# The mask product of the banded heads: identity and band held in one float32r tile, written once by ScalarE

## The reference

```python
def gqa_sink_attend(q, k, v, mask, sinks):
    s = jnp.einsum('bqkgd,bnkd->bkgqn', qg, k).astype(jnp.float32) * (HEAD_DIM ** -0.5)
    if mask is not None:
        s = jnp.where(mask, s, NEG_INF)        # NEG_INF = -1e30
    ...
    p = jax.nn.softmax(jnp.concatenate([s, sink], axis=-1), axis=-1)[..., :-1]
    o = jnp.einsum('bkgqn,bnkd->bqkgd', p.astype(v.dtype), v)
```

## Time and profile before

| | us |
|---|---|
| median of 3 runs | 3647.12 (3645.98 to 3649.39) |
| the profiled execution: its own time | 3649.55 |
| the profiled execution: span | 3647.8 |
| TensorE busy | 3357.4 (92%) |
| VectorE busy | 2337.5 (64%) |
| ScalarE busy | 1849.9 (51%) |

### The profile page before, as it was taken

One profiled execution on the slowest core, in us unless ns is written; L12 is line 12 of the kernel. 1 busy time (PEld: TensorE's weight loads), 2 busy tenths in 40 slices (PEclk: granted clock), 3 DMA queues, 4 the chain that ended last, 5 costly groups with the idle time before them and its releaser, 6 DMA issues.

```text
span 3647.8 us, 56528 instructions
## 1 busy us (share of the span) xinstructions
PE 3357.4 (92%) x24411; PEld 3080.7 (84%) x24411; DVE 2337.5 (64%) x2986; ACT 1849.9 (51%) x2198; POOL 0.2 (0%) x4
## 2 busy tenths in 40 slices
PE   7979999989689899999999999898799979998798
PEld 7968989989689799999999999775577869974598
DVE  6756655567566588888888888534465545555354
ACT  5454444445544377777776776423444434434343
POOL 0000000000000000000000000000000000000000
PEclk9989999999899899999999999997799989999899
DMA  6423455444234599899899998323224355411253
GB/s 248 163 86 114 171 211 193 173 162 152 93 116 171 200 372 352 330 353 349 329 360 336 342 360 324 129 78 127 104 87 157 127 198 184 174 59 58 93 185 116
DMA packets 102671, 723.49 MB, mean 198 GB/s; under 512 B 11664, under 2 KB 13328, under 8 KB 16528
## 3 DMA queue, kind: packets, MB, share of 16 engines
q1 hardware_dynamic: 102416, 719.80, 53.2%
HBM read 718.71 MB, written 1.05 MB: 197 GB/s over the span
## 4 chain that ended last, share of the span: by engine, by line
PE 80%; DVE 9%; ACT 6%; DMA 3%; issue 1%; SPq 0%; DVEq 0%; ACTq 0%
PE PS L1361 14%; PE PS L1362 13%; PE PS L1363 13%; PE PS L1314 6%; PE PS L1312 6%; PE PS L1313 6%; DVE WL L2064 3%; PE PS L1618 3%; PE PS L1616 3%; PE PS L1617 3%; ACT WH L1680 3%; PE PS L1428 3%; PE PS L1457 2%; DMA RAW<-in_ffn_w 1%; PE PS L1391 1%
## 5 line engine op out<-in xcount | busy, mean ns | idle before, releaser
L2064 DVE TENSOR_TENSOR WL<-RAW,WH 128x2048 fp32r<-128x2048 f32 (+3 forms) x428 | 962.9, 2252 | 646.7 <-ACT WH L1680 641.5
L1680 ACT ACTIVATE WH<-RAW 128x2048 fp32r<-128x2048 f32 (+3 forms) x428 | 802.7, 1878 | 270.3 <-PE PS L1363 182.0
L1361 PE MATMUL PS<-PH,WH 128*128 128x256 f32 x2464 | 715.5, 290 | 34.8 <-DVE PL L2236 11.1
L1362 PE MATMUL PS<-PL,WH 128*128 128x256 f32 x2464 | 700.9, 284 | 0.0
L1363 PE MATMUL PS<-PH,WL 128*128 128x256 f32 x2464 | 700.7, 284 | 0.0
L2064 DVE TENSOR_TENSOR WL<-F,WH 128x2048 fp32r<-128x2048 f32 x210 | 481.2, 2292 | 87.5 <-ACT WH L1680 86.5
L1361 PE MATMUL PS<-HPH,WH 128*128 128x256 f32 (+1 forms) x1648 | 496.9, 302 | 41.7 <-DVE WL L2064 27.1
L1361 PEld LDWEIGHTS PS<-PH,WH 128*128 128x128 f32 x2464 | 475.3, 193 | 43.8 <-issue 29.8
L1362 PE MATMUL PS<-HPL,WH 128*128 128x256 f32 (+1 forms) x1648 | 482.4, 293 | 0.0
L1363 PE MATMUL PS<-HPH,WL 128*128 128x256 f32 (+1 forms) x1648 | 482.3, 293 | 0.0
L1362 PEld LDWEIGHTS PS<-PL,WH 128*128 128x128 f32 x2464 | 475.2, 193 | 1.3
(11 more groups left out here) (379 smaller groups left out, 5158.4 us busy)
## 6 DMA issues: line engine op xcount, KB each, us to landing
F<-in_moe_w SPq DMA_DIRECT2D x210, 1024.0 KB, 5.1
RAW<-in_ffn_w SPq DMA_DIRECT2D x130, 1024.0 KB, 4.8
RAW<-in_moe_w SPq DMA_DIRECT2D x126, 1024.0 KB, 4.9
RAW<-in_w_in SPq DMA_DIRECT2D x64, 1024.0 KB, 4.8
F<-in_ada_w SPq DMA_DIRECT2D x18, 1024.0 KB, 11.2
RAW<-in_ada_w SPq DMA_DIRECT2D x18, 1024.0 KB, 5.9
RAW<-in_w_kv SPq DMA_DIRECT2D x16, 1024.0 KB, 4.7
RAW<-in_w_in_ab SPq DMA_DIRECT2D x12, 1024.0 KB, 4.9
```

Source lines behind the costliest of these rows:

```text
L1361: T_.matmul(out, lh, rh, start=first, stop=False)
L1362: T_.matmul(out, lh, rl, start=False, stop=False)
L1680: S.activation(mem["WH"][:, t.s % NHL, 0:m], v.raws[t.slot][:, 0:m], ACT.Copy).then_inc(*ac.done("w_hi", t.s))
L2064: V.tensor_tensor(mem["WL"][:, t.s % NHL, 0:m], v.raws[t.slot][:, 0:m], mem["WH"][:, t.s % NHL, 0:m].bitcast(F32), sub).then_inc(*dv.done( ...
```

## The change

The band gets an input tensor of its own and is no longer part of `CST2`. SyncE loads it into the tile `BIAS`, which no head uses yet. In `lam2` ScalarE waits for it and writes a new tile `BAND` of type float32r: columns 0 to 127 eight times the identity, columns 128 to 639 the band. The banded heads' mask product reads both operands from there as float32r. The neighbourhood heads' product reads the same identity reinterpreted as float32, and stays a float32 product with the float32 bias. The first two bias loads and the first mask or bias product wait for `band_r`. The masked value is -2^100 in place of -1e30. `CST2` shrinks by 640 columns and `BAND`, next to it, has 640.

```diff
-CONSTS2 = [("ident8", 128), ("rot", 128), ("cos", 256), ("sin", 256), ("band", 512)]
+CONSTS2 = [("rot", 128), ("cos", 256), ("sin", 256)]
@@ the loads of the neighbourhood heads' biases
-   after=() if hd > 1 else [("ps", "v", f"d0.{i}") for i in range(4)] + [("ps", "v", f"n0.{i}") for i in range(8)])
+   after=() if hd > 1 else [("ps", "v", f"d0.{i}") for i in range(4)] + [("ps", "v", f"n0.{i}") for i in range(8)] + [("band_r",)])
@@ tensor_program, s
         if spec["bias"]:
+            pe.wait_ge("band_r")
             if spec["kind"] == "near":
                 tile = plan.tile["bias", spec["hd"]]
                 pe.wait_ge(f"land{tile.slot}", tile.turn)
                 b = tile.raw[:, 0, qb * T:qb * T + T]
             else:
-                b = v.C2("band")[:, qb * T:qb * T + T]
-            last = T_.matmul(ps[:, 256:512], v.C2("ident8"), b, start=False, stop=True)
+                b = mem["BAND"][:, 128 + qb * T:128 + qb * T + T]
+            eight = mem["BAND"][:, 0:128]
+            last = T_.matmul(ps[:, 256:512], eight.bitcast(F32) if spec["kind"] == "near" else eight, b, start=False, stop=True)
@@ scalar_program, lam2
     def lam2():
+        ac.wait_ge("band")
+        S.activation(mem["BAND"][:, 0:128], v.C("ident"), ACT.Copy, scale=8.0)
+        S.activation(mem["BAND"][:, 128:640], mem["BIAS"][:, :], ACT.Copy).then_inc(*ac.done("band_r"))
         ac.wait_ge("lam2_s")
@@ sync_program, second
         SP.dma_start(mem["CST2"][:, :], io["cst2"]).then_inc(*sp.done("cst2", by=16))
+        SP.dma_start(mem["BIAS"][:, :], io["band"]).then_inc(*sp.done("band", by=16))
         SP.dma_start(mem["LAMB"][:, :], io["lamb"]).then_inc(*sp.done("lamb", by=16))
@@ build
         mem["CST2"] = sb("CST2", [128, NCST2])
+        mem["BAND"] = sb("BAND", [128, 640], F32R)
@@ constants
-    band = np.concatenate([np.where(np.abs(q * 128 + p[:, None] - j[None, :]) <= 128, 0.0, NEG) for q in range(2)], 1).astype(np.float32)
+    band = np.concatenate([np.where(np.abs(q * 128 + p[:, None] - j[None, :]) <= 128, 0.0, -2.0 ** 100) for q in range(2)], 1).astype(np.float32)
```

More of the change, by code:

```diff
@@ L623, in splits_ahead @@
         if t.after:
-            newest = max(newest, *(at[x[1:]] if x[0] == "ps" and x[1] != "v" else at["pair", "mg1"] if x[1] == "mg1" else -1 for x in t.after))
+            newest = max(newest, *(-1 if x[0] == "band_r" else at[x[1:]] if x[0] == "ps" and x[1] != "v" else at["pair", "mg1"] if x[1] == "mg1" else -1 for x in t.after))
         if t.split:
@@ L2748, in constants @@
     cos, sin = (np.tile(f(ang).T, (2, 1)).astype(np.float32) for f in (np.cos, np.sin))
-    band = np.concatenate([np.where(np.abs(q * 128 + p[:, None] - j[None, :]) <= 128, 0.0, NEG) for q in range(2)], 1).astype(np.float32)
+    band = np.concatenate([np.where(np.abs(q * 128 + p[:, None] - j[None, :]) <= 128, 0.0, -2.0 ** 100) for q in range(2)], 1).astype(np.float32)
     iota = np.concatenate([np.tile(np.arange(128.0), (128, 1)), p[:, None], p[:, None] + 128.0], 1).astype(np.float32)
-    return cst, causal, np.concatenate([ident * 8, rot, cos, sin, band], 1), iota
+    return cst, causal, np.concatenate([rot, cos, sin], 1), band, iota
 def lay_out(x):
@@ L2776, in lay_out @@
     par["ml_rows"] = rows
-    cst, causal, cst2, iota = constants()
+    cst, causal, cst2, band, iota = constants()
     wc = x["w_in_c_2"][0]
@@ L2794, in lay_out @@
     out = {
-        "par": np.concatenate([par[n] for n, _ in VECS], 1), "cst": cst, "causal": causal, "cst2": cst2, "iota": iota,
+        "par": np.concatenate([par[n] for n, _ in VECS], 1), "cst": cst, "causal": causal, "cst2": cst2, "band": band, "iota": iota,
         "xT": packed(x["x"][0].T)[0], "memT": packed(x["mem"][0].T)[0], "ctxT": packed(x["ctx_2"][0].T)[0],
```

## The result

The changed kernel took 3635.37 us (median of 7 runs, 3631.26 to 3639.21), the kernel before 3649.39 us in its 7 runs beside it (3645.98 to 3653.93). The ratio is 0.9962, with a 95% interval from 0.9951 to 0.9974. A second comparison on another chip gave 3635.43 us (12 runs) against 3643.14 us (35 runs), ratio 0.9976 (0.9965 to 0.9986). So the change makes the kernel 0.2 to 0.4% faster, 9 to 14 us; the forecast was 9.8 us. The two intervals overlap. The changed kernel had the same time in both, and the runs of before differ by 6 us; whether that is chance or the chip, no run tells.

A forecast was written before the change was run, and what follows sets the result against it. TensorE, busy 92% of the span, was taken as the bound. 10.9 us saved on mask products, less 0.1 for `lam2` and 1.0 for the clock, gave 9.8 off 3647.12: 3637.3 us, range 3631 to 3644 (forecast case alone 3634 to 3640).

The forecast's parts named there:

- The price of a product: Banded mask product on TensorE: from 0.63 to 0.32 us at full clock, saving 0.31, or 0.65 at the lower clock.
- Rival (a): Banded mask product: float32r alone between float32 products costs more, saving 0.23 us each, 7.4 us, 3640.8 us; chance 0.08.
- (e): Banded mask product still has two records, or its 0.63 us stay: 3647.2 us; chance 0.04.
- All on the path: Banded heads: all 32 mask products stand on the chain, so their 10.9 us of saving counts in full.
- Rival (b): Banded heads: a new wait takes half the gain, leaving 4.3 us, 3642.8 us; chance 0.12.
- The clock: Banded stage: slightly more time at the lower clock takes back 1 us, between nothing and 3.5.
- Rival (c): Banded stage: one stretch of lower clock fewer, gain 14.3 us, 3632.8 us; chance 0.13.
- (d): Banded stage drops to the differential heads' clock; slower, 3654.2 us with six more low-clock stretches; chance 0.05.
- `lam2`: ScalarE's two copies, 0.92 us, go into 0.83 us of idle time ahead of the exponential: 0.1 us added.
- Loads and waits: One more DMA ahead of `lamb` and new waits for `band` and `band_r`: costed at nothing, uncovered some 4 us each.

The follow-up runs named there:

- two multiplied kernels: The runs five float32r and three float32, which issue the banded mask product several times: 3652.74 us, and ratio 1.0064 to the kernel before.
- five float32r: Changed kernel with the banded mask product issued five times instead of once, all float32r: 3652.74 us, ratio 1.0023 to the kernel before.
- again: Same kernel rerun without edit: changed, ratio 0.9976 to before; before, ratio 0.9992; type undone, for its profile, banded stage 159.34 us.
- more copies: Changed kernel with four more ScalarE copies of 128x512 ahead of the two in `lam2`: 3636.04 us, ratio 0.9975.
- near_copies: near_r with all its copies, moves and waits, but the neighbourhood heads' product still float32: 3642.56 us, ratio 1.0.
- near_r: Changed kernel extended to the neighbourhood heads: ScalarE copies each bias to float32r, their 16 products are float32r too: 3638.46 us, ratio 0.9995.
- type undone: Changed kernel with the banded mask product reading BAND as float32 again, copies, loads, waits and mask value kept: 3646.09 us, ratio 1.001.
- -1e30: Changed kernel with the masked value at -1e30 again, rounded to float32r by ScalarE: 3637.48 us, ratio 0.9979.
- mask over 128 columns: Changed kernel with the banded mask product over only the 128 columns holding anything but zero: one profile, 0.26 us on the chain.
- three float32: Changed kernel with the banded mask product in float32 and issued three times: ratio 1.0064 to the kernel before, stage 186.75 us.
- no mask: Changed kernel without the banded heads' mask product at all: 3619.58 us, ratio 0.9931.

## Why the prediction was right

**The price of a product** was right to 0.01 us: 0.315 for 0.32 at the full clock, 0.51 for 0.50 at the lower. The two multiplied kernels gave its parts separately, 0.215 us for a float32 record and 0.117 for a float32r one. The other 0.20 us were there in both kernels; how they divide between the weight load and the change from 64 rows to 128 and back, no run separates. Rival (a), a dearer lone record, is out, and so is (e).

**All on the path** was right. In the first part of the stage, up to 3290 us on the clock of before, neither kernel met the lower clock. Eleven mask products lie there, and the changed kernel was 3.5 us ahead: 11 x 0.315. In the same part five float32r records cost 5.2 us over one (11 x 4 x 0.117), and six float32 records 9.5 us over two (11 x 4 x 0.215), both in full. The chain has 24 of the 32 products in the changed kernel where it had all 32, so a few are now beside VectorE's and ScalarE's steps, but these steps had waited for a product themselves. Rival (b) is out: its 4.3 us lie below both intervals of the gain, and the runs with more records show it from the other side.

**The clock** was the term that I had too small in the profiles of this stage. 10.9 us of work went and the stage got 7.3 us shorter, where I had expected about 10. The granted clock went from 0.91 of 160.5 us to 0.89 of 153.2, and since only the levels 1.2 and 2.4 GHz occur, that is 29 us at the lower one before and 34 after. 5 us more at half speed cost up to 2.5; the traces' own clock marks (27.3 and 34.1 us) make it 3.4. I had allowed 1.0 with 3.5 as the end. It was alike in four profiles of kernels with this stage (153.2 to 153.5 us at 0.89: changed, again, with more copies, near_copies), so it is no single accident, but near_r, whose banded stage has the same TensorE work, had 149.6 us at 0.92. The sign is therefore not a law, and that less work causes more of the lower clock is argued, not shown.

The length of the stage in all these kernels, the time at the lower clock in it by the marks, and the length less half of that time. If TensorE were all that counts, the last column would be the length at the full clock:

| kernel | us | us at the lower clock | length less half of them |
|---|---|---|---|
| before, again | 160.5, 160.5 | 27.3, 27.3 | 146.8, 146.9 |
| type undone, again | 158.1, 159.3 | 20.5, 23.9 | 147.9, 147.4 |
| changed, again | 153.2, 153.3 | 34.1, 34.1 | 136.2, 136.2 |
| more copies, near_copies | 153.3, 153.5 | 34.1, 34.1 | 136.3, 136.4 |
| near_r | 149.6 | 23.9 | 137.7 |
| -1e30 | 151.7 | 30.7 | 136.4 |
| mask over 128 columns | 156.7 | 47.8 | 132.8 |
| five float32r | 165.7 | 27.3 | 152.1 |
| three float32 | 186.75 | 20.5 | 176.5 |
| no mask | 138.8 | 27.3 | 125.2 |

The last column orders the kernels as their records do. The type costs 10.6 to 11.7 us, the 128 float32r records 15.9, the 128 float32 ones 28.6 to 29.1. Where TensorE waits, an us at the lower clock costs less than half of it, so the column is somewhat too short, most where much time is at the lower clock.

The timed runs tell the same for the whole kernel, since each has its span and its mean granted clock on record. Span times clock is the time that would be left if every us at the lower level were halved. Means, each against the runs of before on the same chip, with standard errors:

| kernel | runs | span times clock | us at the lower level |
|---|---|---|---|
| changed | 12 | -9.8 (1.0) | +2.0 (2.8) |
| type undone | 12 | +2.0 (1.0) | +0.6 (3.8) |
| five float32r | 12 | +5.4 (0.9) | +4.2 (2.5) |
| three float32 | 5 | +31.2 (2.7) | -14.2 (6.8) |
| no mask | 5 | -20.4 (1.3) | -10.0 (3.2) |
| near_copies | 11 | -5.6 (1.1) | +11.1 (3.0) |
| near_r | 12 | -13.1 (1.2) | +21.1 (5.1) |

The changed kernel lost 9.8 us of work by this measure, and the lower level took back up to 1.0 us, half of 2.0, with an error of 1.4. The forecast had 1.0. An extra 6.8 us at the lower level, as the profiles have it in the stage, is not ruled out by 2.0 with an error of 2.8, but it isn't confirmed either. Rival (c), a clock in favour, has nothing for it, although its 14.3 us are close to the 13.9 of the first comparison; (d) didn't occur. In near_r the work fell further, by 3.5 us below the changed kernel, but it had 16 us more at the lower level (error 5), worth up to 8, and its mean time was 4.7 us longer (error 2.3).

The Trainium skill's page "TensorE: Matmul & The Clock Gate", section "A second HAM failure mode: psum-queue depth-cycling", agrees with part of this case's traces. In the kernel before the lower clock begins at 3331.0 and 3372.0 us, in the changed one at 3283.0, 3317.1 and 3368.3 us, and the last wait of TensorE ahead of each of these (of those above 0.7 us) was 1.0 to 1.4 us long. But the stage also has one long wait, and the lower clock that begins at 3348.1 us begins inside it:

```profile
3344.04 0.66 PE L1445 MATMUL PS<-CST,G 128*128 128x128 f32 x4
3350.40 0.55 PE L1377 MATMUL PS<-HPH,WH 128*128 128x256 f32 x1 [5.71 <-ACT WH L1680]
```

This one fits the section "HAM oscillation — how this bites in real kernels" of the same page of the Trainium skill. So the traces have both. By the long gaps alone the change would have kept 10.8 us; the stage gave 7.3 in the profiles, and the timed runs with 8.7 to 13.9 can't tell the two apart.

**`lam2`** cost nothing at its own exponential, where I had 0.1. The copies took 0.29 and 0.62 us as worked out, but each starts some 0.1 us before the span ahead of it ends. From the root's end at 2330.26 to the table load at 2330.99 they hold ScalarE for 0.73 us, which fits into the 0.83. The exponential starts 0.03 us after VectorE's sums, as it did before. The stretch from 2290 to 2345 us was slower by 2.4 us in the profile after, but by 0.3 in its second profile. The lower clock held 13.7 us of it, 3.4 more than in the kernel before, which is worth up to 1.7 us. In the type-undone kernel the stretch was 2.8 us slower with no more of the lower clock, and its timed runs lie 2.0 us above before in span times clock. So a price of 1 or 2 us of the copies, loads and waits together is not ruled out, and I had put all but 0.1 us of it at nothing.

**Loads and waits** at nothing: between 2290 and 2345 us no trace shows one of them ending an idle time.

**The sum.** 9.8 us forecast, 13.9 and 8.7 measured, and 9.8 in span times clock. That the last agrees to the tenth is luck, given its error of 1.0. The absolute 3637.3 us (3635.4 measured) rests on a median of three runs of before; other samples of before lay at 3642.6 to 3649.4, a spread of 7 us, larger than any term that I disputed. A single pair of profiles would have been read wrongly: half of its 14.2 us came from a place with no change.

**No version that keeps the mask is shown to beat the changed kernel here.** The neighbourhood heads could give 5 us by the price of their records, if their copies were made well ahead of the score products. That takes a second buffer for them and wasn't tried.

## What to carry to other kernels

Price a matmul from records that stand back to back and count what surrounds it (own weight load, change of row count) apart: the first part scaled with type and columns here, the second stayed at 0.20 us. Where TensorE is the chain, a record removed arrives in full in its work. What the clock adds or takes differs between executions by more than such an edit is worth: in the profiles of this stage a third of the gain was gone, in the timed runs of the whole kernel about a tenth, with an error as large. So judge such an edit by many timed runs with their granted clock, and by several profiles read stage by stage. A conversion is cheap at a place where its engine stands idle for at least its length and nothing on another engine waits for it: two copies fitted into 0.83 us in `lam2`. The 16 copies of 0.4 us placed just ahead of their readers made TensorE wait for 11 us, those runs had more time at the lower clock, and the gain was gone.

## What the hardware showed that was not expected

A float32r record of 128 columns costs 0.26 us alone between float32 products, one of 256 columns 0.315. Before that run I had read the 0.11 us between the gathers' records as a floor, but here the price goes nearly by columns (0.055 us for 128).

The low clock in a stage with unchanged instructions varies between executions: from 2498 to 2600 us thirteen other profiles were 3.4 to 9.1 us shorter than the first of before. The stage of the neighbourhood heads (2700 to 2870 us in the kernel before) had 3.4 us at the lower clock in both profiles of before and both of the changed kernel, and 17.1 in the run with -1e30, where it has the changed kernel's instructions, and was some 6 us longer there. The banded stage alone repeats to 0.1 us in two profiles of before and in three with the changed product, and yet differs by 1.2 us between two profiles of the type-undone kernel.
